# Decays between tokens in a Mamba-2 mixer: triangle stationary, masked step sizes moving as two float32r tables that GpSimd makes

## The reference, cut to what matters

```python
def segsum(a):
    t = a.shape[-1]
    rep = jnp.broadcast_to(a[..., :, None], a.shape + (t,))
    rep = jnp.where(jnp.tril(jnp.ones((t, t), dtype=bool), -1), rep, 0.0)
    ss = jnp.cumsum(rep, axis=-2)
    return jnp.where(jnp.tril(jnp.ones((t, t), dtype=bool)), ss, -jnp.inf)

def ssd_chunked(x, a, bm, cm):
    ...
    a_cs = jnp.cumsum(a, axis=-1)
    decay = jnp.exp(segsum(a))
    cb = jnp.einsum('bclgn,bcsgn->bgcls', cm, bm)
    y_diag = jnp.einsum('bgjcls,bcsgjp->bclgjp', cb[:, :, None] * decay, x)
    ...
```

## Time and profile before

| what | value |
|---|---|
| median of three runs | 1432.09 us |
| span of the profiled execution | 1430.0 us |
| TensorE busy | 1398.2 us (98%) |
| VectorE busy | 1021.1 us (71%) |
| ScalarE busy | 521.8 us (36%) |
| GpSimd busy | 274.9 us (19%) |
| mean granted TensorE clock | 0.999 of 2.4 GHz |

### The profile page before, as it was taken

One profiled execution on the slowest core, in us unless ns is written; L12 is line 12 of the kernel. 1 busy time (PEld: TensorE's weight loads), 2 busy tenths in 40 slices (PEclk: granted clock), 3 DMA queues, 4 the chain that ended last, 5 costly groups with the idle time before them and its releaser, 6 DMA issues.

```text
span 1430.0 us, 23127 instructions
## 1 busy us (share of the span) xinstructions
PE 1398.2 (98%) x9058; PEld 1285.1 (90%) x9058; DVE 1021.1 (71%) x1836; ACT 521.8 (36%) x953; POOL 274.9 (19%) x235
## 2 busy tenths in 40 slices
PE   8999999999999999999999999999999999999998
PEld 7788889999999999999999998888889978888886
DVE  5566747989888886544444527788789897687887
ACT  5545464311433332000000006444457586544444
POOL 1000036344255454433333300000000000000000
PEclk9999999999999999999999999999999999999999
DMA  6445444699999999999999985555444333455552
GB/s 235 177 147 179 175 154 156 220 415 408 367 369 377 371 364 394 416 415 414 417 414 415 414 345 181 205 199 181 176 165 168 125 106 111 167 203 194 187 194 89
DMA packets 67211, 372.13 MB, mean 260 GB/s; under 512 B 7969, under 2 KB 8481, under 8 KB 34866
## 3 DMA queue, kind: packets, MB, share of 16 engines
q1 hardware_dynamic: 37440, 266.45, 49.0%
q0 software_dynamic: 27648, 100.68, 18.0%
q10 hardware_dynamic: 2034, 3.76, 0.7%
HBM read 369.81 MB, written 1.05 MB: 259 GB/s over the span
## 4 chain that ended last, share of the span: by engine, by line
PE 67%; DVE 14%; DMA 10%; ACT 6%; issue 3%; POOL 0%; DVEq 0%; SPq 0%; ACTq 0%; POOLq 0%
PE ps L754 26%; PE ps L1064 11%; PE ps L787 11%; PE ps L1013 10%; DMA raw<-in_experts 9%; PE ps L789 5%; ACT xt_plain L1527 3%; DVE wlo L569 2%; DVE hi_plain L2087 2%; DVE xt_plain L2201 2%; DVE lo_plain L2087 2%; DVE arena L2190 1%; DVE XT L1897 1%; PE ps L786 1%; DVE arena L2512 1%
## 5 line engine op out<-in xcount | busy, mean ns | idle before, releaser
L1064 PE MATMUL ps<-arena,raw 128*128 128x160 f32 x2048 | 282.1, 300 | 6.5 <-DMA raw<-in_experts 6.4
L1064 PEld LDWEIGHTS ps<-arena,raw 128*128 128x128 f32 x2048 | 278.6, 190 | 9.9 <-issue 6.0
L1013 PE MATMUL ps<-arena,raw 128*128 128x160 f32 x2048 | 284.8, 300 | 2.1 <-DVEq L2182 0.9
L1013 PEld LDWEIGHTS ps<-arena,raw 128*128 128x128 f32 x2048 | 279.2, 190 | 4.8 <-issue 2.1
L787 PE MATMUL ps<-XT,whi 128*128 128x512 f32 x704 | 249.5, 399 | 1.2 <-DVE wlo L569 1.0
L552 ACT ACTIVATE whi<-raw 128x1024 fp32r<-128x1024 f32 x152 | 159.7, 1060 | 237.5 <-PE ps L754 108.8
L569 DVE TENSOR_TENSOR wlo<-raw,whi 128x1024 fp32r<-128x1024 f32 x138 | 167.2, 1221 | 81.1 <-ACT whi L552 80.2
L754 PE MATMUL ps<-whi,XT 128*128 128x512 f32 x592 | 184.8, 393 | 3.3 <-DVE XT L1897 1.5
L789 PE MATMUL ps<-XT,wlo 128*128 128x256 f32 x616 | 172.8, 281 | 0.0
L1621 ACT ACTIVATE whi<-raw 128x1024 fp32r<-128x1024 f32 x96 | 101.9, 1062 | 155.7 <-PE ps L787 101.6
L787 PEld LDWEIGHTS ps<-XT,whi 128*128 128x128 f32 x704 | 129.4, 188 | 28.3 <-DVE wlo L569 2.1
(11 more groups left out here) (312 smaller groups left out, 1861.4 us busy)
## 6 DMA issues: line engine op xcount, KB each, us to landing
raw<-in_experts SPq DMA_DIRECT2D x128, 1024.0 KB, 8.0
raw<-in_panels SPq DMA_DIRECT2D x58, 1024.0 KB, 4.9
raw<-in_ffa SPq DMA_DIRECT2D x33, 1024.0 KB, 4.9
raw<-in_ffb SPq DMA_DIRECT2D x33, 1024.0 KB, 4.8
arena<-in_row_post ACTq DMA_DIRECT2D x4, 512.0 KB, 4.9
X<-in_x SPq DMA_DIRECT2D x2, 512.0 KB, 5.3
hi_plain<-in_peer_u,arena POOLq DMA_INDIRECT x48, 9.0
lo_plain<-in_peer_u,arena POOLq DMA_INDIRECT x48, 9.9
```

What stands on the lines that cost most here:

```text
L1013: last = pe.matmul(out[:, 0:TD], w[:, k], XF[:, k, :], start=k == 0, stop=k == NK - 1)
L1064: last = pe.matmul(t_bank("ffa", k // 2)[:, at:at + TD], w[:, P * k:P * k + P], G[:, c, :], start=False, stop=False, skip_group_check=True)
```

## The change

The sums are made the other way round. The triangle is now the stationary operand, rounded to float32r (`after_gt`, a copy of `MGT`, exact since it holds zeros and ones). The moving operand is a table of masked step sizes: `MLE` times the step size of each token and head. So that float32r is exact enough, the step sizes are split into a high part (`ADH`) and a rest (`ADL`), and there are two tables for each chunk. A bank of four heads is then the sum of two matmuls with 512 moving columns in place of four float32 matmuls with 128.

The four tables are made by GpSimd, one after another, as soon as `ad_ready` comes. The two instructions of VectorE that made the tables are gone. VectorE gets two small ones (the rounded copy and the rest), which stand ahead of `ad_ready`. The tables lie over parts of the arena that are used later (`Z`, `PR`, `AOUT`).

```diff
@@ sizes and places
+        arena_at = nc.sbuf_base
         arena = sb("arena", [P, P * T])
+        ROUND_AT = 8224
+        arena_r = nc.alloc_sbuf_tensor_at("arena_r", [P, P * T - ROUND_AT], f32r, offset=arena_at + 4 * ROUND_AT)
...
+        ADL = cut(NT, SSM_H)
...
+        adh = rounded(NT * SSM_H)
+        ADH = adh.bitcast(f32).rearrange("p (t h) -> p t h", t=NT)
+        after_gt = rounded(P)
...
-        TA = [TA0, Cut(at_aout)(SSM_H, P)]
+        TA = [[rounded(SSM_H * P, at) for at in ats]
+              for ats in ((at_ta0, at_z), (at_aout, at_pr + 3072))]
@@ GpSimd, at the end of its list
+            pool.wait_ge(pool_const2, 9)
+            pool.tensor_copy(after_gt, MGT).then_inc(pool_const2, 1)
+            pool.wait_ge(ad_ready, 1)
+            for c in range(2):
+                for part, steps in zip(TA[c], (ADH, ADL)):
+                    pool.tensor_tensor(part.rearrange("p (h l) -> p h l", h=SSM_H),
+                                       MLE.unsqueeze(1).broadcast_to([P, SSM_H, P]),
+                                       steps[:, c, :].unsqueeze(2).broadcast_to([P, SSM_H, P]), ALU.mult)\
+                        .then_inc(ta_ready, 1)
@@ TensorE
             def between_tokens(c):
-                pe.wait_ge(ta_ready, c + 1)
+                pe.wait_ge(pool_const2, 10)
+                pe.wait_ge(ta_ready, 2 * c + 2)
                 for q in range(4):
                     claim(pe, f"ss{4 * c + q}")
-                    for j in range(4):
-                        last = pe.matmul(bank(f"ss{4 * c + q}")[:, P * j:P * j + P], TA[c][:, 4 * q + j, :], MLE,
-                                         start=True, stop=True)
+                    for n, part in enumerate(TA[c]):
+                        last = pe.matmul(bank(f"ss{4 * c + q}"), after_gt, part[:, 512 * q:512 * q + 512],
+                                         start=n == 0, stop=n == 1)
                     last.then_inc(main_done, 1)
@@ VectorE
-            ins.then_inc(ad_ready, 1)
+            link(ins)
+            link(dve.tensor_copy(adh, AD.rearrange("p t h -> p (t h)")))
+            dve.tensor_tensor(ADL, AD, ADH, ALU.subtract).then_inc(ad_ready, 1)
...
-            for c in range(2):
-                split_to(S_AQ + 2 + c)
-                dve.tensor_tensor(TA[c], MGT.unsqueeze(1).broadcast_to([P, SSM_H, P]),
-                                  AD[:, c, :].unsqueeze(2).broadcast_to([P, SSM_H, P]), ALU.mult).then_inc(ta_ready, 1)
+            split_to(S_AQ + 3)
```

More of the change, by code:

```diff
@@ L405, in program @@
         SSTATE = cut(2, 512)
+        at_ta0 = cut.at
         TA0 = cut(SSM_H, P)
@@ L408, in program, with rounded @@
         DTT = cut(T)
+        ADL = cut(NT, SSM_H)
+        def rounded(n, at=None):
+            at = cut.at if at is None else at
+            cut.at = max(cut.at, at + n)
+            return arena_r[:, at - ROUND_AT:at - ROUND_AT + n]
+        adh = rounded(NT * SSM_H)
+        ADH = adh.bitcast(f32).rearrange("p (t h) -> p t h", t=NT)
+        after_gt = rounded(P)
         prf = PR.rearrange("p a b c -> p (a b c)")
@@ L412, in program @@
         at_aout = 2048 + XC * (T + CONVW - 1) + XC * T + 2048 + 2048 + 1024 + 4096 + 6144
-        TA = [TA0, Cut(at_aout)(SSM_H, P)]
+        at_z = 2048 + XC * (T + CONVW - 1) + XC * T
+        at_pr = at_aout - 6144
+        TA = [[rounded(SSM_H * P, at) for at in ats]
+              for ats in ((at_ta0, at_z), (at_aout, at_pr + 3072))]
         W = [XN2.rearrange("p a b -> p (a b)").rearrange("p (h s) -> p h s", h=SSM_H), TA0]
```

## The result

| | before | after |
|---|---|---|
| median of runs, us | 1432.44 (1431.9 to 1434.66, 4 runs) | 1445.17 (1442.81 to 1446.68, 4 runs) |
| span of the profiled execution, us | 1430.0 | 1443.3 |
| ratio after / before | | 1.0093, 95% interval 1.0081 to 1.0106 |

The change makes the kernel 12.7 us slower (forecast 16.9, to 1449.0). The two profiled executions differ by 13.3 us.

A forecast was written before the change was run, and what follows sets the result against it. It took TensorE and VectorE, sharing the stage with nearly no slack, as the bound. 0.45 + 17.9 + 1.5 - 3.0 = +16.9 us on a 1430.0 span, 1449.0 us as median; own range 1443 to 1454, 8-in-10 range 1438 to 1458.

The forecast's parts named there:

- Step 1: Decay-sum matmuls on TensorE: each chunk falls from 3.6 to 1.84 us, -3.0 us together after a wait for keys.
- Step 2: Tables leaving VectorE (L2460, 4.49 us at 1110.20): credited with nothing, at best 0.3 us.
- Step 3: Two small chained VectorE instructions ahead of `ad_ready`, on the chain: +0.45 us, bounds 0.3 and 0.6.
- Step 4: GpSimd's tables (4.75 us each) and VectorE's two-SBUF-input instructions exclude each other from 1087.45 on: +17.9 us.
- rival C: Broadcast operand slow on GpSimd, 7.1 us a table: 1458.5; other end, 1.73 us a table: 1437; chance 0.09.
- Step 5: TensorE's first matmuls after its long wait run at 1.2 GHz: +1.5 us, half of a bound of 2.9.
- A: VectorE's runs keep GpSimd out; each table costs 4.15 us, no clock term: +14 us, 1446; chance 0.09.
- B: GpSimd hardly gets in before 1110, so tables come late and hold VectorE's key parts: +6 us, 1438; chance 0.05.
- D: No lock between GpSimd and VectorE, only the matmul saving counts: -2.6 us, 1429.5; chance 0.07.

The follow-up runs named there:

- a: The changed kernel with all four tables made by VectorE and none by GpSimd: 1434.91 us, ratio 1.0018.
- j: The changed kernel with 10 and 47 unused identity matmuls in TensorE's two pauses, reaching up to VectorE's late part: 1441.99 us, ratio 1.0071.
- k: As i, with VectorE's third and fourth key parts split ahead of an instruction of the skip term: 1429.95 us, ratio 0.9984.
- l: As a, plus four unused GpSimd products and subtractions of 1024 numbers, on one operand read twice or two different ones: 1444.21 us.
- h: The changed kernel with 10 and 38 unused identity matmuls in TensorE's two pauses: 1442.84 us, ratio 1.0077.
- e: The changed kernel with GpSimd waiting for the last convolution block before making the four tables: 1439.91 us, ratio 1.0061.
- d: The changed kernel without the low parts: GpSimd makes two tables, TensorE runs one matmul a bank: 1437.19 us, ratio 1.0031.
- g: As a, plus four unused products of 2048 numbers (plain, broadcast, table, plain) and two copies on GpSimd: 1447.25 us.
- i: The changed kernel with high tables made by VectorE and low ones by ScalarE, none by GpSimd: 1430.7 us, ratio 0.9988.
- f: As a, plus six unused GpSimd fills of 2560 numbers that write SBUF and read nothing: 1434.52 us, ratio 1.0015.
- c: The changed kernel with each GpSimd table made in four instructions of 512 numbers, sixteen in all: 1442.55 us, ratio 1.0073.

## Why the prediction was right, and where it was off

The direction, the mechanism and the order of the terms hold; the time is 3.8 us too high, inside the forecast's own range (1443 to 1454). That it lies well inside is partly luck. The range was built on a table of 4.3 to 5.4 us, and a table took 3.4; the terms measured in the stage, put on the same 1432.09, give 1443.3, at the very edge.

- **What bounds the kernel.** Right. The stage had next to no slack on VectorE: it lost 2.66 + 9.91 = 12.57 us to GpSimd, and 12.2 arrived at TensorE. a and j show it by taking the lock or the clock away alone.
- **Step 1, matmuls, -3.0.** Measured -2.7. Chunk 1 takes 1.86 us (forecast 1.84) and gives 1.7. Chunk 0 takes 2.15 (TensorE's timeline of after, 1133.16 to 1135.31; 2.16 in k), and the view of its line has a weight load waiting 0.4 us for ScalarE (L1716), which the step left out. Then comes the wait for the third key part that the step named, 0.3 us where it had 0.6. Chunk 0 gives 1.0, forecast 1.2.
- **Step 2, tables leave VectorE, 0.** After's VectorE has 4.21 us of idle time ahead of L2517, before 0.48: in after, the 4.49 us bought nothing. That fits the 0, though no run takes L2460 alone away.
- **Step 3, +0.45.** Measured 0.44.
- **Step 4, the lock, +17.9.** The mechanism is right to the instruction: table 1 holds L587, tables 2, 3 and 4 hold L2462 no. 1, 2 and 3. The mis-sized term is the table, forecast at 4.75 us, twice the 2.38 of 1024 split numbers. Measured, without VectorE's turns (0.44 to 1.14 us), the four are 3.61, 3.45, 3.35 and 3.34 us, 3.44 on average. Four times 1.3 is 5.2 of the 5.7 us that the term is too high (12.2 in place of 17.9); most of the rest is the 0.4 us that VectorE lost and TensorE did not feel. The table lay between the taken value and the fast end that I bounded by the fill (1.73), and rival C, a slow broadcast, had the wrong sign. What made the row a bad price is half settled: l shows 0.15 to 0.3 us per 1024 for a second full operand, which a table, whose operands repeat, does not pay. The other 0.3 (2.38 against 2.05) stays open; the operands' places in SBUF and ScalarE writing beside are untested. The Trainium skill (GPSIMD Engine Reference, "Instruction dispatch") has a floor of about 2.5 cycles a number for two inputs. At the 1.2 GHz that the same page of the Trainium skill gives ("Specifications"), 3.44 us for 2048 are 2.0 cycles, below that floor; the measurement decides. By it the term would have been 1.9 us lower than mine and still too high.
- **Step 5, the clock, +1.5.** Measured 1.3, and j shows it by itself. It was half of a bound, so the closeness is partly luck: in the other runs the same fall cost 1.5 (h, e), 2.2 (l, 22.60 us for 168) and 2.5 (d). d's pause was the shorter one, 3.92 us against 9.20, and cost more, because the lower clock lasted longer behind it (some 5 us, in after some 3). What sets that is open.
- **Rivals.** A is excluded by the timeline: GpSimd gets in behind each single instruction, while VectorE has a queue of them. Its sum also put the clock at nothing because TensorE's pauses would be under 4.2 us; in after a pause of 2.43 us was enough for a clock of 0.50, and in d one of 3.92. B is excluded for the same reason; all tables were done by 1105.25. C's slow side is excluded by after's tables (3.4 us) and by g. D is excluded by after itself: no instruction of VectorE with two SBUF operands ran through while GpSimd made a table.
- **The sum.** 0.44 + 12.2 + 1.3 - 2.7 = 11.25 us in the stage, and 2.1 us of scatter ahead of it make the 13.3 of the two profiled executions. The medians say 12.7; the 1.5 us between that and the stage are not placed, and they are no more than the medians of these kernels scatter against their stages (a +1.8, h -1.2).

## What to carry to other kernels

Work moved to an idle GpSimd is free only if VectorE has slack in that stretch or works on PSUM there. In these runs, while GpSimd read SBUF, each of its instructions let exactly one of VectorE's instructions with two SBUF inputs by, and cutting its work into shorter pieces changed little. Read the stretch, not the page: GpSimd had 20% of the span and nothing of the chain, and caused all of the loss. The idle time of ScalarE was the better place: VectorE kept its own speed beside it (i).

## What the runs showed of the hardware that I had not expected

- Fills by GpSimd hold nothing of VectorE (f: 13.73 us beside 2.71); copies with one input do (g: some 1.6 us each), and a VectorE instruction with an operand in PSUM passes (e: 0.68).
- The turns are strict. Behind every GpSimd instruction one of VectorE's with two SBUF inputs ran, never two, whether it was 0.45 or 1.14 us long (after, c, g).
- GpSimd took 1.7 ns a number for a table (after, 3.44 us for 2048), 1.7 to 1.9 for one operand read twice and 2.0 for two different ones (l), 2.32 in L569, and VectorE 1.1 (a).
- A pause of TensorE of 2.08 us behind a run of identity matmuls was followed by two microseconds at the lower clock (h), and so was one of 2.43 us behind the matmuls of a weight part (after); without the pauses there was none (j). But the length alone does not decide: in d, too, TensorE stood for 2.43 us (up to 1093.69), and the clock of 1090 to 1095 is 1.00. A longer pause did not cost more: 2.5 us behind 3.92 (d), 1.3 behind 9.20 (after).
